# Rotary half swap of queries and keys: a VectorE row shuffle in place of a TensorE permutation matmul

## What is computed

```
q = partial_rope(rms_norm(z_q, att_q_norm), pos)      # k likewise
# partial_rope, half = 16:
x1, x2 = x[..., :16], x[..., 16:32]
out = [x1 * cos - x2 * sin,  x2 * cos + x1 * sin,  x[..., 32:]]
```

## Time and profile before

| | |
|---|---|
| times of the runs | 1660.37, 1662.29 (median) and 2834.34 us |
| profiled execution, first to last instruction (span) | 1658.5 us |
| PE busy | 1577.8 us, 95% of the span |
| DVE busy | 975.1 us, 59% |
| ACT busy | 594.7 us, 36% |
| POOL busy | 125.9 us, 8% |
| mean granted TensorE clock | 0.974 of full speed |
| HBM | 254.65 MB read, 8.56 MB written, 159 GB/s over the span |

### The profile page before, as it was taken

One profiled execution on the slowest core, in us unless ns is written; L12 is line 12 of the kernel. 1 busy time (PEld: TensorE's weight loads), 2 busy tenths in 40 slices (PEclk: granted clock), 3 DMA queues, 4 the chain that ended last, 5 costly groups with the idle time before them and its releaser, 6 DMA issues. The chain is left out here.

```text
span 1658.5 us, 29883 instructions
## 1 busy us (share of the span) xinstructions
PE 1577.8 (95%) x10908; PEld 1423.0 (86%) x10908; DVE 975.1 (59%) x1384; ACT 594.7 (36%) x827; POOL 125.9 (8%) x168
## 2 busy tenths in 40 slices
PE   5999999799999999999989999997999999999998
PEld 4999999566967679999989999985597775999997
DVE  5766557865644437665466664678565353666643
ACT  4333344033523134343353333432343221443331
POOL 3000000702001101000000000006200001000000
PEclk7999999799999999999999999999999999999999
DMA  7565554245455537564455655442555555465542
GB/s 225 157 171 158 165 166 153 77 128 191 149 175 204 174 130 198 154 175 160 146 144 163 170 153 178 154 133 78 183 178 160 171 178 178 127 177 157 171 159 99
DMA packets 310010, 263.95 MB, mean 159 GB/s; under 512 B 7096, under 2 KB 292024, under 8 KB 309882
## 3 DMA queue, kind: packets, MB, share of 16 engines
q1 hardware_dynamic: 290242, 203.14, 40.7%
q0 software_dynamic: 13776, 48.97, 8.7%
q10 hardware_dynamic: 5896, 10.54, 2.1%
HBM read 254.65 MB, written 8.56 MB: 159 GB/s over the span
## 5 line engine op out<-in xcount | busy, mean ns | idle before, releaser
L1336 PE MATMUL pairs<-h_hi,w_hi 128*128 128x288 f32 x1824 | 545.1, 299 | 13.0 <-DVE h_lo L862 10.8
L1336 PE MATMUL pairs<-h_hi,w_lo 128*128 128x288 f32 x1824 | 542.7, 298 | 0.0
L1336 PE MATMUL pairs<-h_lo,w_hi 128*128 128x288 f32 x1824 | 542.6, 297 | 0.0
L859 DVE TENSOR_TENSOR w_lo<-raw_weights,w_hi 128x1024 fp32r<-128x1024 f32 (+1 forms) x388 | 450.3, 1202 | 136.6 <-ACT w_hi L636 133.6
L636 ACT ACTIVATE w_hi<-raw_weights 128x1024 fp32r<-128x1024 f32 (+1 forms) x388 | 381.6, 1032 | 292.5 <-PE pairs L1336 283.3
L1336 PEld LDWEIGHTS pairs<-h_hi,w_hi 128*128 128x128 f32 x1824 | 345.9, 190 | 18.0 <-DVE h_lo L862 11.4
L1336 PEld LDWEIGHTS pairs<-h_lo,w_hi 128*128 128x128 f32 x1824 | 346.3, 190 | 0.4
L1336 PEld LDWEIGHTS pairs<-h_hi,w_lo 128*128 128x128 f32 x1824 | 345.4, 189 | 0.0
L1336 PE MATMUL pairs<-g_hi,w_lo 128*128 128x288 f32 x704 | 208.4, 296 | 0.0
L1336 PE MATMUL pairs<-g_lo,w_hi 128*128 128x288 f32 x704 | 208.3, 296 | 0.0
L1336 PE MATMUL pairs<-g_hi,w_hi 128*128 128x288 f32 x704 | 207.8, 295 | 0.0
(11 more groups left out here) (267 smaller groups left out, 1696.9 us busy)
## 6 DMA issues: line engine op xcount, KB each, us to landing
raw_weights<-in_w_ffn_in SPq DMA_DIRECT2D x176, 512.0 KB
raw_weights<-in_w_ffn_out SPq DMA_DIRECT2D x32, 1024.0 KB
raw_weights<-in_w_in SPq DMA_DIRECT2D x18, 1024.0 KB
mem_kv<-in_cache_mem_k POOLq DMA_DIRECT2D x16, 1024.0 KB, 5.3
raw_weights<-in_w_ckv SPq DMA_DIRECT2D x16, 1024.0 KB
raw_weights<-in_w_ffn_out SPq DMA_DIRECT2D x16, 768.0 KB
raw_weights<-in_w_out SPq DMA_DIRECT2D x8, 1024.0 KB
raw_weights<-in_w_cq SPq DMA_DIRECT2D x8, 1024.0 KB
```

The lines of the kernel that those rows point to most:

```text
L859: return dve.tensor_tensor(out, in0, in1, op)
L1336: return pe.matmul(out, lhsT, rhs, start=start, stop=stop, **kw)
```

## The change

The permutation matmul and its four turns are taken out of PE's program and of `MIX_ORDER`. DVE makes the swapped rows itself, with a shuffle of 32 partitions from `z` to `rope_tmp`, a drain, and the multiply by `sin2` now from `rope_tmp` instead of from PSUM. On PE, `att_turned(0)` now follows `win(7)` at once. DVE's wait for ACT's count of `att_k[0]` moves from the third rope pair to the first `att_s` turn. The semaphore `z_normed`, on which only the matmuls waited, goes. The number of turns falls by four, so all the turns that stay keep their buffer.

```
-MIX_ORDER = (... ["qk_root"] * 4 + ["win"] + ["rope"] * 2 + ["att_k"] + ["rope"] * 2 + ["att_s", "att_k", "att_s"]
+MIX_ORDER = (... ["qk_root"] * 4 + ["win"] + ["att_k", "att_s", "att_k", "att_s"]
 ROPE_ORDER = (0, 2, 1, 3)
+ROPE_SWAP = [(_i + ROPE_DIM // 2) % ROPE_DIM for _i in range(ROPE_DIM)]
 # DVE
-                for place, j in enumerate(ROPE_ORDER):
-                    if place == 2:
-                        dve.wait_ge(acc_free, passed(L, 0, TURNS["att_k"][0]))
-                        dve.sem_inc(dve_passed, 1)
-                    pair = acc(L, TURNS["rope"][place])
-                    turned = z[0:ROPE_DIM, 2 * j:2 * j + 2, :]
-                    free(tt(rope_tmp[0:ROPE_DIM, :, :], pair[0:ROPE_DIM, :, 0:T], sin2, ALU.mult))
+                for j in ROPE_ORDER:
+                    turned, swapped = z[0:ROPE_DIM, 2 * j:2 * j + 2, :], rope_tmp[0:ROPE_DIM, :, :]
+                    dve.stream_shuffle(swapped, turned, ROPE_SWAP)
+                    dve.drain()
+                    tt(swapped, swapped, sin2, ALU.mult)
                     tt(turned, turned, cos2, ALU.mult)
                     dve.drain()
-                    tt(turned, turned, rope_tmp[0:ROPE_DIM, :, :], ALU.add).then_inc(z_done, 1)
+                    tt(turned, turned, swapped, ALU.add).then_inc(z_done, 1)
                     dve.drain()
                 spread_q(dve, att=True)
                 for j in range(2):
-                    if j == 1:
-                        dve.wait_ge(acc_free, passed(L, 0, TURNS["att_k"][1]))
+                    dve.wait_ge(acc_free, passed(L, 0, TURNS["att_k"][j]))
 # PE
                 win(7)
-                for place, j in enumerate(ROPE_ORDER):
-                    pair = take(L, TURNS["rope"][place])
-                    pe.wait_ge(z_normed, L * 4 + j + 1)
-                    for e in range(2):
-                        ins = mm(pair[0:ROPE_DIM, e, 0:T], cc("swap"), z[:, 2 * j + e, :])
-                    ins.then_inc(acc_ready, 1)
-                    if place == 1:
-                        att_turned(0)
                 for j in range(2):
-                    if j == 1:
-                        att_turned(1)
+                    att_turned(j)
                     pair = take(L, TURNS["att_s"][j])
```

More of the change, by code:

```diff
@@ L82 @@
 CX_ORDER += ["ckv", "ckv", "mkt", "mkt", "ckv", "cx_s", "cx_s", "ckv", "cx_pt", "cx_pt", "cx_o", "cx_o", "cx_so"]
-MIX_ORDER = (["state_in"] + ["win"] * 6 + ["qk_stat", "win"] + ["qk_root"] * 4 + ["win"] + ["rope"] * 2 + ["att_k"] + ["rope"] * 2 + ["att_s", "att_k", "att_s"]
+MIX_ORDER = (["state_in"] + ["win"] * 6 + ["qk_stat", "win"] + ["qk_root"] * 4 + ["win"] + ["att_k", "att_s", "att_k", "att_s"]
              + ["att_k"] * 2 + ["win"] + ["att_k"] * 2 + ["att_pt"] * 2 + ["att_k"] * 2 + ["tok"] * 3 + ["pool", "state_out"]
@@ L275, in trunk_kernel @@
         x_rounded, m_rounded = sem("x_rounded"), sem("m_rounded")
-        gate_ready, zsq_ready, rq_ready, z_normed, z_done = (
-            sem(n) for n in ("gate_ready", "zsq_ready", "rq_ready", "z_normed", "z_done"))
+        gate_ready, zsq_ready, rq_ready, z_done = (
+            sem(n) for n in ("gate_ready", "zsq_ready", "rq_ready", "z_done"))
         mixer_idle, mixer_params, states_in = sem("mixer_idle"), sem("mixer_params"), sem("states_in")
@@ L1065, in _ @@
                     stt(z[:, 2 * j:2 * j + 2, :], z[:, 2 * j:2 * j + 2, :], par("att_q_norm" if j < 2 else "att_k_norm"), pair[:, :, 0:T],
-                        ALU.mult, ALU.mult).then_inc(z_normed, 1)
+                        ALU.mult, ALU.mult)
                     free(dve.drain())
@@ L1071, in _ @@
                 free(scaled(v_t[:, 0:2, :], win(7, 15, 19)[:, :, 0:T]))
-                for place, j in enumerate(ROPE_ORDER):
-                    if place == 2:
-                        dve.wait_ge(acc_free, passed(L, 0, TURNS["att_k"][0]))
-                        dve.sem_inc(dve_passed, 1)
-                    pair = acc(L, TURNS["rope"][place])
-                    turned = z[0:ROPE_DIM, 2 * j:2 * j + 2, :]
-                    cos2 = ap(const, COLS["cos"][0], [[0, 2], [1, T]], ROPE_DIM)
-                    sin2 = ap(const, COLS["sin"][0], [[0, 2], [1, T]], ROPE_DIM)
-                    free(tt(rope_tmp[0:ROPE_DIM, :, :], pair[0:ROPE_DIM, :, 0:T], sin2, ALU.mult))
+                cos2 = ap(const, COLS["cos"][0], [[0, 2], [1, T]], ROPE_DIM)
+                sin2 = ap(const, COLS["sin"][0], [[0, 2], [1, T]], ROPE_DIM)
+                for j in ROPE_ORDER:
[3 more added lines that the diff above has]
+                    tt(swapped, swapped, sin2, ALU.mult)
                     tt(turned, turned, cos2, ALU.mult)
                     dve.drain()
-                    tt(turned, turned, rope_tmp[0:ROPE_DIM, :, :], ALU.add).then_inc(z_done, 1)
+                    tt(turned, turned, swapped, ALU.add).then_inc(z_done, 1)
                     dve.drain()
@@ L1088, in _ @@
                 for j in range(2):
-                    if j == 1:
-                        dve.wait_ge(acc_free, passed(L, 0, TURNS["att_k"][1]))
-                        dve.sem_inc(dve_passed, 1)
+                    dve.wait_ge(acc_free, passed(L, 0, TURNS["att_k"][j]))
+                    dve.sem_inc(dve_passed, 1)
                     pair = acc(L, TURNS["att_s"][j])
```

## The result

The changed kernel takes 1671.43 us (median of 4 runs, 1669.85 to 1671.85), the kernel before 1662.29 (median of three, 1660.37 to 1663.03; the one run of 2834.34 stands far off and is left out). The ratio is 1.0054, 95% interval 1.0039 to 1.0069: **slower by about 9 us, half a per cent**, well inside the two per cent within which the prediction saw the change with 0.95. The forecast was 1671 within 1661 to 1680. The profiled execution took 1671.54 us and spans 1670.0, 11.5 more than the one before.

A forecast was written before the change was run, and what follows sets the result against it. It took DVE's rotation, then PE without slack, as the bound: 8.0 us for both layers plus 2.5 for the clock, 10.5, on a 1658.5 us span, plus about 2 for ordinary runs, gave 1671 us, range 1661 to 1680.

The forecast's parts named there:

- The path: From win(7) to the second att_s DVE's rotation sets the pace, then PE carries any delay on without slack.
- The shuffle: Four added DVE shuffles of 32 x 576 per layer, 0.74 us each plus 0.07 drain: 3.2 us per layer.
- POOL: Multiply by sin2, now with both inputs in SBUF, is slowed beside POOL: 1.0 us per layer, half the possible 2.0.
- the full case: Every multiply by sin2 slowed by 0.51 us, 2.0 per layer; as rival with permutation loads 1675 us, chance 0.13.
- The sum per layer: Per layer, shuffles and drains 3.2, less 0.2 removed, plus 1.0 for POOL: 4.0 us, 8.0 for both.
- the sign: First shuffle to q_diag copy: about 18 to 19 us in the first layer, 15.5 to 17 in the second.
- The matmuls: Removing PE's permutation matmuls, 11.7 us over both layers, gains only one small DVE wait, 0.2 us per layer.
- The clock: After a longer PE wait, second layer's second att_s and first sample scores run at the low clock: 2.55 us lost.
- the terms that I costed at nothing: The struck semaphore and turns, the earlier att_turned(0), ACT copy and page loads, and DVE's moved wait: each zero.

The follow-up runs named there:

- twice: The changed kernel with every row shuffle and its drain done twice; 1676.79 us beside 1661.09 for the kernel before.
- after_inc: The changed kernel with the four normalising DVE instructions counting up z_normed again; 1674.60 us beside 1661.40 for the kernel before.
- before_nopool: The kernel before without POOL's convolution of the 32 new tokens, their columns set to zero; 1653.09 us beside 1661.09 for the kernel before.
- warm: The changed kernel with idle matmuls on PE, 21 ahead of the first att_s and 12 ahead of the second; 1667.34 us beside 1660.64.

## Why the prediction was right

1. **The path.** DVE's rotation, then PE without a gap: shown by twice (6.6 of 7.0 us), and by the delay that stands unchanged from the second `att_s` to the output projection in the first layer.
2. **The shuffle.** 0.74 us forecast, 0.782 measured; its permutation load takes 0.014 us. With drain and load it is 0.87 us from start to next start, against 0.81 forecast: 0.5 us over all eight. The estimate worked out from the Trainium skill (VectorE: DVE Perf Modes, the perf-mode tier table), 0.68, was further off.
3. **POOL.** 2.0 us forecast for both layers; the 24 operations hold 28.4 - 24 x 0.745 = 10.5 us of it, the 16 before 20.0 - 11.9 = 8.1: 2.4 us more. The multiply by `sin2` went from 743 to 1063 ns, 0.32 and not the 0.51 of the full case; taking half was about right for this kernel. That is partly luck: in after_inc, where DVE and POOL meet otherwise, these multiplies took 1320 ns, 0.58 more, and the 24 operations 30.7 us, so the same term is 4.7. The sum per layer was 4.0 us; the rotations grew by 4.66 and 4.01. The first took 19.72 us, above the 18 to 19 that I had named as the sign, the second 16.45, within 15.5 to 17.
4. **The matmuls.** Costed at 0.2 us of gain per layer. Nothing in the runs speaks for more in this kernel. Had POOL not stretched the rotation, DVE would have waited longer ahead of the third turn (1.6 us over both layers in before_nopool, put down to ACT's count of `att_k[0]`), and the gain would have been larger.
5. **The clock.** 2.55 us forecast for the second layer, 2.61 measured from `att_s` to `att_pt`, nothing in the first layer; warm gives both layers back and shows the cause. The forecast took the length of the last wait as the sign. That alone does not decide the level: in before_nopool the second `att_s` ran low behind 1.78 and 1.79 us (2.79 and 2.92 us), and in the kernel before at the high level behind 1.78.
6. **What was not in the sum.** The count of `z_normed` was not free. It belongs to the terms that I costed at nothing, and by after_inc its striking was worth some 4 us in the change's favour. Without it the change would have cost about 13 us, where 9 were forecast (1671 against 1662.3), so the total came out right by luck for those 4 us. Two smaller losses stand in no term either: about 2 us behind the second output projection, where the clock now starts low, and 0.8 from the start-up.

## What to carry to other kernels

Read the busy share in the stretch where the change lies: this kernel is 95% PE, yet the change moved work from an idle PE to a busy DVE. These DVE operations were cheaper beside a working POOL with one operand in PSUM (0.75 us against 1.04 and 1.06). The shuffle, which frees the rotation from PE's turns, paid only where the rotation was then also started earlier, and work that fills an engine's gap must not bring instructions to the engine that makes the gap.

## What the runs showed of the hardware

- A shuffle of 32 x 576 f32 took 773 to 821 ns from SBUF to SBUF and 743 to 751 from SBUF to PSUM, over all these runs.
- 0.02 us per instruction, from counting a semaphore, moved the emptying of `win(7)` by 1.9 us and the kernel by about 4, by the order in which DVE and POOL meet. From the second layer's reciprocal to that emptying it took 25.15 us in before, before_nopool and after_inc; without the count 23.25, in five kernels. It looks like a chance of this program's timing, not a price of counting: in the first layer the same gap is 25.2 us with and without the count.
- The clock at the first matmuls of the output projection swapped layers. PEclk in the first 6 us was 0.71 (first layer) and 1.00 (second) before, and 1.00 and 0.72 after; at the low level the matmuls start 0.24 us apart instead of 0.13, about 1.5 us in all each time. The last waits in front of it are the same in all four, 0.88 and 0.92 us; what sets the level is not shown. The two shifts cancel over the layers: the changed kernel comes up from 5.08 to 3.55 us behind the kernel before in the first layer's projection, and drops from 9.74 to 11.2 behind in the second's. A trace of one layer alone would show a gain or a loss that is none. The first layer's gain did not last: 1.0 us of it went at the start of the second layer, where PE waits 7.42 us instead of 6.50.

```profile
394.20:400.00 5.80, 5.76 (x32) 5.77 (x32) 2.36 (x2) 0.00 (x0) 0.00 (x0) 0.71 0.92 367
1205.10:1211.00 5.90, 5.82 (x43) 5.83 (x44) 2.36 (x2) 0.00 (x0) 0.00 (x0) 1.00 0.99 362
```

```profile
399.30:405.00 5.70, 5.68 (x42) 5.69 (x43) 2.36 (x2) 0.00 (x0) 0.00 (x0) 1.00 0.92 369
1214.90:1221.00 6.10, 6.08 (x34) 6.09 (x35) 2.36 (x2) 0.00 (x0) 0.00 (x0) 0.72 0.91 359
```

```profile
845.20 0.61 PE L1336 MATMUL pairs<-h_hi,w_hi 128*128 128x288 f32 x1 [6.50 <-DVE h_lo L862]
850.00 0.61 PE L1334 MATMUL pairs<-h_hi,w_hi 128*128 128x288 f32 x1 [7.42 <-DVE h_lo L863]
```
